# Modulation weights by output columns in the opening of a one-core two-block network, with single waits placed anew

## What is computed

```
sh1, sc1, g1, sh2, sc2, g2 = split(silu(c) @ ada_w + ada_b, 6)      # c: latent; c_ctx: context
h   = rms_norm(x, g) * (1 + sc1) + sh1                              # per feature, 768 tokens
p   = concat(h_ctx, h_lat) @ w_in                                   # 32 items of 128 columns, "k", "rk", ...
...                                                                 # delta rule, retention, output, SwiGLU
```

## Time and profile before

| | |
|---|---|
| median of 3 runs | 3351.11 us (3349.87 to 3354.0) |
| the profiled execution, its own time | 3351.78 us |
| its span | 3349.9 us |
| TensorE busy | 3284.4 us, 98% |
| VectorE, ScalarE, GpSimd busy | 35%, 41%, 45% |
| read from memory | 318.19 MB |

### The profile page before, as it was taken

One profiled execution on the slowest core, in us unless ns is written; L12 is line 12 of the kernel. 1 busy time (PEld: TensorE's weight loads), 2 busy tenths in 40 slices (PEclk: granted clock), 3 DMA queues, 4 the chain that ended last, 5 costly groups with the idle time before them and its releaser, 6 DMA issues.

```text
span 3349.9 us, 45392 instructions
## 1 busy us (share of the span) xinstructions
PE 3284.4 (98%) x16642; PEld 2760.3 (82%) x16642; DVE 1188.7 (35%) x1886; ACT 1379.3 (41%) x1996; POOL 1517.5 (45%) x1118
## 2 busy tenths in 40 slices
PE   6999999999999999999999999999999999999998
PEld 4778898888888888888888888888888888888887
DVE  5864885111231116444134111411045452161104
ACT  4544555443254323256225342444233363254423
POOL 2333113545455544545544454455445444455544
PEclk8999999999999999999999999999999999999999
DMA  7342002332232222223222323232323223223223
GB/s 269 132 151 70 1 1 82 107 99 96 88 98 96 97 98 89 95 88 107 95 82 94 100 94 99 84 100 94 98 85 101 95 95 101 88 89 97 97 95 100
DMA packets 90033, 322.15 MB, mean 96 GB/s; under 512 B 9776, under 2 KB 12208, under 8 KB 89776
## 3 DMA queue, kind: packets, MB, share of 16 engines
q1 hardware_dynamic: 88576, 316.65, 28.7%
q10 hardware_dynamic: 1328, 3.67, 0.3%
HBM read 318.19 MB, written 2.10 MB: 96 GB/s over the span
## 4 chain that ended last, share of the span: by engine, by line
issue 41%; POOL 31%; PE 22%; DVE 4%; DMA 1%; POOLq 1%; ACT 0%; SPq 0%; DVEq 0%; ACTq 0%
POOL w_lo L487 31%; PE ps L548 4%; PE ps L549 4%; PE ps L553 4%; DMA ada_first<-ada 1%; PE ps L893 1%; PE ps L1142 1%; PE ps L1147 1%; PE ps L1140 1%; PE ps L922 1%; PE ps L568 1%; PE ps L1004 1%; DVE inverse_span L2017 0%; PE ps L1164 0%; PE ps L1166 0%
## 5 line engine op out<-in xcount | busy, mean ns | idle before, releaser
L487 POOL TENSOR_TENSOR w_lo<-raw,w_hi 128x512 fp32r<-128x512 f32 x1086 | 1483.2, 1388 | 1694.9 <-ACT w_hi L1312 1694.9
L1312 ACT ACTIVATE w_hi<-raw 128x1024 fp32r<-128x1024 f32 x543 | 576.1, 1061 | 1415.1 <-PE ps L553 867.7
L548 PE MATMUL ps<-acts,w_hi 128*128 128x512 f32 x2776 | 1080.2, 389 | 0.9 <-ACT tmp L1719 0.7
L549 PE MATMUL ps<-acts,w_hi 128*128 128x512 f32 x2776 | 1080.0, 389 | 0.0
L553 PE MATMUL ps<-acts,w_lo 128*128 128x512 f32 x2776 | 685.5, 389 | 0.0
L548 PEld LDWEIGHTS ps<-acts,w_hi 128*128 128x128 f32 x2776 | 521.1, 188 | 109.5 <-ACT tmp L1719 1.7
L549 PEld LDWEIGHTS ps<-acts,w_hi 128*128 128x128 f32 x2776 | 521.2, 188 | 108.0
L553 PEld LDWEIGHTS ps<-acts,w_lo 128*128 128x128 f32 x2776 | 521.1, 188 | 108.1
L2341 DVE TENSOR_TENSOR tmp<-tmp,ps 128x512 f32<-128x512 f32 x110 | 75.7, 688 | 787.4 <-PE ps L553 727.7
L1140 PE MATMUL ps<-acts,w_hi 128*128 (+1 forms) x440 | 171.2, 389 | 0.0
L1142 PE MATMUL ps<-acts,w_hi 128*128 (+1 forms) x440 | 171.2, 389 | 0.0
(11 more groups left out here) (391 smaller groups left out, 3963.6 us busy)
## 6 DMA issues: line engine op xcount, KB each, us to landing
raw<-stream SPq DMA_DIRECT2D x543, 512.0 KB, 3.3
ada_behind<-ada SPq DMA_DIRECT2D x32, 512.0 KB, 3.8
ada_first<-ada SPq DMA_DIRECT2D x8, 1024.0 KB, 12.6
X<-x_in ACTq DMA_DIRECT2D x1, 2048.0 KB, 8.6
out<-X SPq DMA_DIRECT2D x16, 128.0 KB, 2.1
xin<-x_in ACTq DMA_DIRECT2D x2, 768.0 KB, 6.8
xin<-x_in SPq DMA_DIRECT2D x2, 768.0 KB, 9.0
rope_sb<-rope SPq DMA_DIRECT2D x1, 1280.0 KB, 9.9
```

Source lines behind the costliest of these rows:

```text
L487: last = nc.gpsimd.tensor_tensor(w_lo[:, slot, part, :], raw[:, slot % RAW, part, :], f32(w_hi[:, slot, part, :]), ALU.subtract)
L548: mm(o, w_hi[:, s, k, :], xh, start=start, stop=False, skip_group_check=True)
L549: mm(o, w_hi[:, s, k, :], xl, start=False, stop=False, skip_group_check=True)
L1312: A(w_hi[:, s, :, :], raw[:, s % RAW, :, :], ACT.Copy).then_inc(s_hi, 1)
```

## The change

The two modulation parts that the first features need are computed by output columns. On the host, `ada_w`'s parts 0 and 1 are laid out as four slices of 256 columns (feature tiles 2q and 2q+1), each with all 1024 rows: one 1 MB transfer for the shift and one for the scale. `slice_part` multiplies one of them (eight matmuls; row block k goes to quarter k % 4 of the array). The result, four partial sums on rows 0, 32, 64, 96, is copied out whole and `turn_slice` multiplies it with a matrix of selected ones, which sums and turns it. `slice_cols` forms `mod` and `coef` for two tiles, and these two feature tiles follow at once. x is no longer multiplied by the root in a pass of its own: one instruction does scale times root (line 1908 of the changed kernel), ScalarE adds the shift as it rounds, and VectorE adds it again in the low part. Slices 2 and 3 and three of the four turns stand on TensorE inside `first_items`. The squares go to eight buffers, start when the first half of x is there, and TensorE sums four pair sums. The first two weight chunks are loaded ahead of `ada_first` and split before the root.

The other edits move single waits. The turn of a later part stands one item later. For items 0 and 1 ScalarE reads the banks before it splits chunks. `ret_variances` stands at the end of steps 0 and 1 of the delta rule and not inside steps 1 and 2. An Ln ahead of time loads ScalarE's table. `opening` takes the fourth chunk of k = 0 last. `gelus` reads the second bank before it splits. In `norm` the residual of a half stands ahead of the sum of the square before it.

```diff
@@ sync @@
-            for n in range(N_PROJ + 1):
-                if n >= RAW:
-                    sp.wait_ge(s_lo, split.up())
+            for n in range(RAW, N_PROJ + 1):
+                sp.wait_ge(s_lo, split.up())
...
+            def slice_part(q, part):
+                n, bank = 2 * q + part, ps[(6, 4)[q % 2] + part]
+                pe.wait_ge(s_first[n % FIRST], 16 * (n // FIRST + 1))
+                if part == 0 and q == 1:
+                    pe.wait_ge(s_std0, 1)
+                if part == 0 and q > 1:
+                    pe.wait_ge(s_part, q - 1)
+                for k in range(KT):
+                    g = 32 * (k % 4)
+                    last = mm(bank[g:g + 32, 0:2 * P], cond[:, k, :], ada_first[:, n % FIRST, 2 * P * k:2 * P * (k + 1)],
+                              start=(k < 4), stop=(k >= 4), skip_group_check=True)
+                last.then_inc(s_ada, 2)
+            def turn_slice(q):
+                pe.wait_ge(s_arow, q + 1)
+                for part in range(2):
+                    bank = ps[(6, 4)[q % 2] + part]
+                    for a in range(2):
+                        last = mm(bank[:, 2 * P + 2 * a:2 * P + 2 * a + 2],
+                                  slices[:, q % 2, part, a * P:(a + 1) * P], zeta[:, 0:2], start=True, stop=True)
+                last.then_inc(s_acol, 1)
...
@@ first_items, between w_hi and w_lo of tile k @@
+                    if k in (0, 2, 3):
+                        turn_slice((1, 0, 2, 3)[k])
...
@@ first_items, behind tile k @@
+                    if k < 2:
+                        slice_part(2, k)
+                    elif k == 2:
+                        for part in range(2):
+                            slice_part(3, part)
...
@@ scalar @@
+            for j, k in enumerate(SQUARED):
+                if j % 4 == 0:
+                    act.wait_ge(s_xl[j // 4], 32)
+                A(sqs[:, k, :], xin[:, k, :], ACT.Square).then_inc(s_sq, 1)
+            for _ in range(RAW):
+                hi_part()
...
+                for v, tokens in ((1, slice(0, CTX)), (0, slice(CTX, TOK))):
+                    last = A(h1[:, k, 0, tokens], big[k % 2][:, tokens], ACT.Identity, bias=mod[:, k, v:v + 1])
...
-                TS(b[:, 0:CTX], xin[:, k, 0:CTX], coef[:, 1, k:k + 1], mod[:, k, 1:2], ALU.mult, ALU.add)
+                        last = STT(big[k % 2][:, tokens], xin[:, k, tokens], coef[:, v, k:k + 1], big[3][:, tokens],
+                                   ALU.mult, ALU.mult)
...
+                        last = STT(h1[:, k, 1, tokens], big[k % 2][:, tokens], mod[:, k, v:v + 1],
+                                   f32(h1[:, k, 0, tokens]), ALU.add, ALU.subtract)
...
-                    if i in TURNS:
-                        turn_part(TURNS[i], 7)
+                    if i - 1 in TURNS:
+                        pe.wait_ge(s_part, SLICES + TURNS[i - 1] - 2)
+                        turn_part(TURNS[i - 1], 7)
...
@@ opening @@
-                    for j in range(SLOTS):
+                    for j in range(SLOTS - (k == 0)):
                         high_low(j, k)
+                    if k == 0:
+                        pe.wait_ge(s_hi, n_hi.up())
...
+                        high_high(SLOTS - 1, k)
+                        high_low(SLOTS - 1, k)
...
@@ gelus @@
-                        done()
+                        act.wait_ge(s_done, used.up())
+                        if j == 0:
+                            hi_part()
...
@@ vector, the delta rule @@
-                    if s in (1, 2) and lev == 1:
-                        ret_variances(2 * (s - 1))
...
+                        if d and s < 2:
+                            ret_variances(2 * s)
...
@@ norm, i >= n.lead @@
-                    if i < KT - 1:
-                        if rows:
-                            add_row(i, HALVES[0])
-                        add_square(i, i, HALVES[0])
+                    if rows and i < KT - 1:
+                        add_row(i, HALVES[0])
+                    add_square(i - 1, i - 1, HALVES[0] if i > n.lead else slice(0, LAT))
```

More of the change, by code:

```diff
@@ L381, in build @@
         s_xhi = sem("xhi")
-        s_xin = sem("xin")
+        s_xl = [sem(f"xl{i}") for i in range(2)]
         s_xlo = sem("xlo")
@@ L580, in turn_part @@
                 last.then_inc(s_acol, 1)
-            pe.wait_ge(s_csil, 1)
-            for n in range(KT - 2):
-                part_chunk(n, 0)
-            pe.wait_ge(s_cst, 32)
-            pe.wait_ge(s_sqadd, KT)
-            mm(ps[4][:, 0:CTX], ones[:, :], big[2][:, 0:CTX], start=True, stop=True)
-            mm(ps[5][:, :], ones[:, :], big[2][:, CTX:TOK], start=True, stop=True).then_inc(s_ss, 1)
-            for n in range(KT - 2, KT + 4):
-                part_chunk(n, n // KT)
-            turn_part(0, 6)
@@ new lines, in turn_slice @@
+            def turn_slice(q):
[6 more added lines that the diff above has]
+                last.then_inc(s_acol, 1)
+            pe.wait_ge(s_cst, 32)
+            for j, k in enumerate(SQUARED[::2]):
+                pe.wait_ge(s_sqadd, j + 1)
+                mm(ps[4][:, 0:CTX], ones[:, :], sqs[:, k, 0:CTX], start=(j == 0), stop=(j == 3), skip_group_check=True)
+                last = mm(ps[5][:, :], ones[:, :], sqs[:, k, CTX:TOK], start=(j == 0), stop=(j == 3),
+                          skip_group_check=True)
@@ L596, in first_items @@
+            last.then_inc(s_ss, 1)
+            pe.wait_ge(s_csil, 1)
+            for part in range(2):
+                slice_part(0, part)
+            turn_slice(0)
+            for part in range(2):
+                slice_part(1, part)
             def first_items():
@@ L1827, in part_cols @@
                    ALU.add).then_inc(s_part, 1)
-                dve.wait_ge(s_part, part + 1)
-            dve.wait_ge(s_prm, 16)
-            part_rows(0, 0)
-            dve.wait_ge(s_std0, 1)
-            for k in range(KT):
-                last = TT(xin[:, k, :], xin[:, k, :], big[3][:, 0:TOK], ALU.mult)
-            link(last)
-            part_cols(0, 6)
-            part_rows(1, 1, count=2)
-            part_cols(1, 7)
-            for j in range(2):
-                last = STT(coef[:, j, :], mod[:, KT:2 * KT, j], 1.0, prm[:, C_GMIX:C_GMIX + KT], ALU.add, ALU.mult)
@@ L1841, in _ @@
-            link(last)
-            for k in range(KT + 1):
-                b = big[k % 2]
-                if k < KT:
+                dve.wait_ge(s_part, SLICES + part - 2 + 1)
+            dve.wait_ge(s_cst, 32)
+            for j in range(2):
+                last = TT(zeta[:, 2 * j:2 * j + 2], ident[:, 64 * j:64 * j + 2], ident[:, 64 * j + 32:64 * j + 34], ALU.add)
+            link(last)
+            link(TT(zeta[:, 0:2], zeta[:, 0:2], zeta[:, 2:4], ALU.add))
+            dve.wait_ge(s_ada, 4)
@@ new lines, in _, with slice_cols @@
+            for part in range(2):
+                last = CP(slices[:, 0, part, :], ps[6 + part][:, 0:2 * P])
+            last.then_inc(s_arow, 1)
+            def slice_cols(q):
+                dve.wait_ge(s_acol, q + 1)
+                for part in range(2):
+                    m = slice(KT * part + 2 * q, KT * part + 2 * q + 2)
+                    last = TT(mod[:, m, :], ps[(6, 4)[q % 2] + part][:, 2 * P:2 * P + 4].rearrange("p (m v) -> p m v", v=2),
+                              prm[:, C_ADAB + m.start:C_ADAB + m.stop].unsqueeze(2).to_broadcast([P, 2, 2]), ALU.add)
+                link(last)
+                for j in range(2):
+                    last = STT(coef[:, j, 2 * q:2 * q + 2], mod[:, m, j], 1.0, prm[:, C_GMIX + 2 * q:C_GMIX + 2 * q + 2],
+                               ALU.add, ALU.mult)
+                last.then_inc(s_part, 1)
+                dve.wait_ge(s_part, q + 1)
@@ L1845, in _ @@
+            parts = ((1, slice(0, CTX)), (0, slice(CTX, TOK)))
+            dve.wait_ge(s_prm, 16)
+            for q in range(KT // 2):
+                slice_cols(q)
+                if q == 0:
+                    dve.wait_ge(s_std0, 1)
+                for k in (2 * q, 2 * q + 1):
                     if k > 1:
                         dve.wait_ge(s_h1, k - 1)
-                    TS(b[:, 0:CTX], xin[:, k, 0:CTX], coef[:, 1, k:k + 1], mod[:, k, 1:2], ALU.mult, ALU.add)
-                    TS(b[:, CTX:TOK], xin[:, k, CTX:TOK], coef[:, 0, k:k + 1], mod[:, k, 0:1], ALU.mult,
-                       ALU.add).then_inc(s_hval, 1)
@@ L1857, in _ @@
+                for k in (2 * q, 2 * q + 1):
+                    dve.wait_ge(s_hhi, k + 1)
+                    for v, tokens in parts:
+                        last = STT(h1[:, k, 1, tokens], big[k % 2][:, tokens], mod[:, k, v:v + 1],
+                                   f32(h1[:, k, 0, tokens]), ALU.add, ALU.subtract)
+                    last.then_inc(s_h1, 1)
             n = len(items)
```

124 lines of the change are left out of this document (60 added, 64 removed).

## The result

| | before | changed |
|---|---|---|
| median (4 runs each) | 3351.8 us (3349.87 to 3354.0) | **3330.59 us** (3330.14 to 3332.85) |
| ratio | | 0.9936, 95% interval 0.9924 to 0.9948 |
| the profiled execution, its span | 3351.8, 3349.9 | 3330.14, 3328.4 |

Faster by 21.2 us where the sum said 17.5. A later series of five gave 3330.77 (3329.14 to 3332.16, ratio 0.9943), beside 3349.84 for the kernel before. So medians of different series can differ by 1 to 2 us without any edit. The range 3328 to 3341 holds the result, the likeliest case's own range (3331 to 3338) just does not. One execution of the later kernel `items_undone` took 3644 us at a granted clock of 0.85 and is left out.

What follows compares the result with a forecast made beforehand. TensorE, busy 98% of the span, was taken as the bound, so only its waits or lower clock yield gains. Terms of 9.1 + 2.4 + 1.2 + 1.8 + 1.1 + 0.9 + 0.7 + 0.3 = 17.5 us gave 3334, range 3328 to 3341.

Steps and rivals of the forecast that it cites:

- more than forecast: Rival for the whole kernel: no clock loss, first and other norms' gains whole; 3329 us, chance 0.08.
- one of its own signs of being wrong: In the changed profile, TensorE's waits for `slices` or `h1` summing to over 4 us would show the prediction wrong.
- Transfers, root, slice (1 to 3): Opening: 1 MB transfers land from 17.4 to 35.4 us, root at 23.7, first slice's matmuls 20.2 to 22.3, chain ends 25.4.
- First product (4): Opening, first tiles: 3.5 us for two tiles after 25.4, so the first product starts at 28.9 against 44.35.
- Stretch (5): First products: 23.6 us of TensorE work plus 2.0 for the clock, ending at 54.5; the opening gives 9.1 us.
- the VectorE rival: VectorE bounds the first products: 7 us per pair instead of 5.9, gain 4.6 us less, 3339 us; chance 0.14.
- Items (6): Items: the 0.6 us bank wait goes and the later turn takes the 1.8 us wait behind `arow`; 2.4 us.
- ret_variances (7): Delta rule, steps 1 and 2: 0.8 us of `keys_state` plus 0.4 behind it; 1.2 us gained (0 to 1.5).
- First norm (8): Residual is freed, but TensorE then waits for the running sum, no earlier than about 550.0; 1.8 of 3.4 us gained.
- Other norms (9): Two other such norm waits, 2.1 us together, decided by the same running sum; 1.1 us gained, bounds 0 and 2.1.
- gelus (11): At `gelus`: a gain of 0.7 us.
- The slow rivals: Half clock through the first products: 3352 us, no change, chance 0.04; another 13 us of it: slower, chance 0.02.

Runs made afterwards that it cites:

- items_undone: Changed kernel with ScalarE again splitting a chunk ahead of emptying the banks of items 0 and 1; 3329.73, 3329.99 and 3333.31 us.
- small_undone: Changed kernel with ret_variances, the fourth chunk's place in opening, gelus and the early table load as before; 3332.84 us, ratio 0.9944.
- late_parts: Changed kernel with the splits of chunks 2 and 3 both behind the eighth tile, not behind the sixth and eighth; 3328.1 us, ratio 0.9931.
- later_only: Kernel before with only the later edits (norm sums, ret_variances, fourth chunk, gelus, early table load); 3346.14 us, ratio 0.9984.
- three_edits: Changed kernel with late splits of chunks 2 and 3, tile 0 begun on its high part, and 3 and 2 filler matmuls; 3329.9 us.
- sum_quads: Changed kernel with VectorE adding the squares by fours, so TensorE multiplies two sums by ones instead of four; 3332.26 us, ratio 0.9945.

## Why the prediction came out as it did

The sign was right, and the range held the time; the forecast 3334 was 3.4 too slow. What happened is nearest to the rival **more than forecast** (0.08 against 0.60): no loss of clock in the profiled execution, and points 8 and 9 nearly whole. In part this is luck: 4.6 us of the gain at later places (2.1 + 1.5 + 1.0) came without the edits that I had credited with it, and nothing in the prediction foresaw that. And one of its own signs of being wrong came true: TensorE's waits for `slices` and `h1` sum to 4.6 us (1.0 and 3.6), over the 4 named, because of the wait at the seventh tile.

- *Transfers, root, slice (1 to 3).* Right within 0.5: TensorE's sums end at 19.9 (20.2), the root at 23.3 (23.7), the slice's matmuls run 19.9 to 21.8 (20.2 to 22.3), the fourth 1 MB transfer is waited for until 25.01 (25.1). `coef` is there at 24.42, not 25.4: the copies, turn and small steps took 2.6 us where I had 3.1, and began 0.5 earlier.
- *First product (4).* 27.99 against 28.9, the difference all from `coef`; the 3.5 us for two tiles were 3.57.
- *Stretch (5).* The end, 54.05 against 54.5, is right with wrong parts, so by luck. The work is 24.3 us (23.6). The clock's 2.0 was not lost in this execution; where it was (`small_undone`, `items_undone`) it was 1.5. In its place stands the wait of 1.73 us at the seventh tile: the VectorE rival came true in one pair of four, where a low part met the tile instructions, and `late_parts` shows that this was its cause. The gap-free forecast "below 1 us between tiles" was wrong there.
- *Items (6).* 3.2 against 2.4: the bank gave 0.7, the first turn 2.1, and small steps at the later turns 0.4.
- *ret_variances (7).* 1.3 against 1.2, confirmed by undoing it.
- *First norm (8): the step that failed.* "The running sum is no earlier than 550.0" took the last split's place relative to TensorE as fixed. It stood 1.8 us earlier in the changed kernel, as its transfer took 3.2 us and not 4.8, and the wait of some 1.3 us forecast for 533 is not there. On the kernel before, where the place is as in the earlier trace rows, the forecast is right to 0.2 us (`later_only`: 1.49 us of new wait, 1.9 gained with the clock full). In the changed kernel the order is worth 1.3, and 2.1 came with the opening alone.
- *Other norms (9).* 2.0 against 1.1: 1.5 came without the edit, 1.3 of it at the norm whose transfer had taken 5.3 us. *Openings (10).* 1.4 against 0.9: 0.7 for each of the two. *gelus (11).* 1.0 against 0.7, 0.4 of it the edit's. *Table load (12).* Nothing, its lower bound.
- *The slow rivals.* The clock that stays half did not come up in any trace with the new opening: the three falls there (`small_undone`, `items_undone`, `three_edits`) each lasted little over 3.3 us. The rule of the Trainium skill, TensorE: Matmul & The Clock Gate, part 1, held as cited: short waits brought the clock down and products brought it back. Its further remark that the moment of the change differs from run to run is what the traces show too: the third pair sum is already fast in the changed kernel (0.59 us at 17.20) and still slow in `items_undone` (1.06 at 17.96), over the same instructions.

## What to carry to other kernels

A wait that stands behind a transfer hangs on the moment as well as on the order of instructions. Look at what else was on the queues during that transfer (here a packet of code), price the edit from both positions of the transfer, and test it alone and undone, since the two answers can differ (here 1.9 and 1.3 us at the first norm, 1.0 and 0.4 at `gelus`). Where an opening was bound by waits and becomes tight, look next for helpers that collide, here GpSimd's low part beside VectorE's tile instructions, and move the one that nobody waits for.

## What the runs showed of the hardware

- The same opening ran with the first product at 27.4 to 29.2 us, depending on how many of the four pair sums had passed before the clock rose. In `items_undone` the third pair is still slow (1.06 us for its 256-column part, 0.59 in the changed kernel) and the product comes 1.2 us later.
- Waits of 1.8 to 2.3 us cost a fall of the clock in one execution and none in another: 1.82 with a fall in `later_only`, the same wait without one in the kernel before; 1.91 without in the changed kernel, 2.31 with one in `small_undone`, 2.32 without in `sum_quads`; in `three_edits` 1.01 with one. So the length of the last wait alone does not decide it. A fall cost 1.5 us (`later_only`, `small_undone`).
- Two VectorE instructions of 2 columns took 1.07 us instead of 0.23 while GpSimd wrote a low part. Two additions with one input in PSUM took 0.23 beside it and 0.22 without.
- A 512 KB transfer took 4.8 us instead of 3.2 from issue to landing where a 16 KB packet of the kind "instruction" fell into it, and this came back in the same place in `later_only` (4.9).
